# Residual input turned by DMA ahead of time instead of by TensorE; another order of VectorE's steps in the output projection; wider row sums

## The reference, cut to what matters

```
h = rmsnorm(x) ; all projections = h @ w_in
branch a: short convolution ; branch b: windowed attention ; branch c: attention over the top 256 keys
merged = sig(g_a)*br_a + sig(g_b)*br_b + sig(g_c)*br_c
x = x + merged @ w_out                 # output projection and residual
h2 = rmsnorm(x)
x = x + (silu(conv(h2 @ w_gate)) * (h2 @ w_up)) @ w_down
y = rmsnorm(x)                         # row by row, output in rows
```

## Time and profile before

| | |
|---|---|
| Time, median of 3 runs | 1747.86 us (1747.72 to 1748.6) |
| The profiled execution's own time | 1749.35 us |
| Its span in the trace | 1747.6 us |
| PE busy | 1716.7 us, 98% |
| DVE, ACT, POOL busy | 77%, 43%, 33% |
| Granted TensorE clock, mean | 0.998 |
| DMA engines busy, over the whole span | 27% |

### The profile page before, as it was taken

The page is one execution under the profiler, slowest core; times in us unless marked ns, Lnnn a source line. Parts: engine busy times, 40 slices in busy tenths (PEclk is TensorE's granted clock), DMA queues, the critical chain, the costliest instruction groups (busy, mean ns, idle before and its releaser), DMA issues.

```text
span 1747.6 us, 32318 instructions
## 1 busy us (share of the span) xinstructions
PE 1716.7 (98%) x12275; PEld 1676.9 (96%) x12275; DVE 1345.7 (77%) x2193; ACT 757.3 (43%) x1333; POOL 580.1 (33%) x466
## 2 busy tenths in 40 slices
PE   6999999999999999999999999999999999999998
PEld 6999999999999999888899999999999999999998
DVE  6689899978799996778659989676666665865765
ACT  5344333378621234767734563333333333422334
POOL 2211842266645431000021102655455554121030
PEclk9999999999999999999999999999999999999999
DMA  4111111110243415422324112222222223533212
GB/s 157 49 26 42 50 43 48 49 41 26 72 133 127 125 40 171 144 85 85 109 71 150 49 49 61 87 84 76 74 80 79 87 74 107 171 117 112 62 37 100
DMA packets 179190, 146.43 MB, mean 84 GB/s; under 512 B 10140, under 2 KB 149676, under 8 KB 179052
## 3 DMA queue, kind: packets, MB, share of 16 engines
q1 hardware_dynamic: 178076, 142.54, 26.2%
q0 software_dynamic: 976, 2.00, 0.5%
HBM read 118.22 MB, written 26.28 MB: 83 GB/s over the span
## 4 chain that ended last, share of the span: by engine, by line
PE 87%; DVE 5%; ACT 2%; POOL 2%; issue 2%; DMA 1%; SPq 0%; DVEq 0%; ACTq 0%; POOLq 0%
PE ps L1602 28%; PE ps L2079 23%; PE ps L2152 7%; PE ps L2138 7%; PE ps L1775 4%; PE ps L1795 4%; PE ps L1614 4%; PE ps L2009 3%; PE ps L1921 3%; PE ps L1869 1%; POOL w_lo L1332 1%; PE ps L1714 1%; POOL w_raw_in_lo L1345 1%; PE ps L1876 1%; DMA w_raw<-in_w_in 1%
## 5 line engine op out<-in xcount | busy, mean ns | idle before, releaser
L3178 DVE MAX8 top<-key_mask 128x8 f32<-128x1024 f32 (+5 forms) x166 | 151.9, 917 | 9.7 <-DVE key_mask L3178 3.4
L1602 PE MATMUL ps<-h_hi,w_hi 128*128 128x352 f32 (+1 forms) x720 | 158.0, 327 | 0.0
L1602 PE MATMUL ps<-h_hi,w_lo 128*128 128x352 f32 (+1 forms) x720 | 155.2, 323 | 0.0
L1602 PE MATMUL ps<-h_lo,w_hi 128*128 128x352 f32 (+1 forms) x720 | 154.8, 323 | 0.0
L1289 POOL TENSOR_TENSOR w_lo<-w_raw,w_hi 128x512 fp32r<-128x512 f32 (+1 forms) x43 | 79.3, 1845 | 216.9 <-ACT w_hi L2246 216.9
L3178 DVE MATCH_REPLACE8 key_mask<-top,key_mask 128x1024 f32<-128x1024 f32 (+5 forms) x166 | 149.5, 904 | 0.3 <-issue 0.3
L2079 PE MATMUL ps<-mix_hi,quarter_hi 128*128 128x264 f32 x672 | 136.9, 285 | 0.3 <-ACT x_one L2246 0.3
L2079 PE MATMUL ps<-mix_hi,quarter_lo 128*128 128x264 f32 x672 | 136.4, 284 | 0.0
L2079 PE MATMUL ps<-mix_lo,quarter_hi 128*128 128x264 f32 x672 | 136.0, 284 | 0.0
L1602 PEld LDWEIGHTS ps<-h_hi,w_hi 128*128 128x128 f32 (+1 forms) x720 | 120.6, 187 | 2.6 <-issue 0.9
L1602 PEld LDWEIGHTS ps<-h_hi,w_lo 128*128 128x128 f32 (+1 forms) x720 | 122.5, 186 | 0.5
(11 more groups left out here) (452 smaller groups left out, 5018.1 us busy)
## 6 DMA issues: line engine op xcount, KB each, us to landing
w_raw<-in_w_in SPq DMA_DIRECT2D x54, 256.0 KB, 3.1
w_hi<-gate_highs SPq DMA_DIRECT2D x48, 256.0 KB, 2.8
w_lo<-gate_lows SPq DMA_DIRECT2D x48, 256.0 KB, 3.0
ffn_tiles<-t SPq DMA_DIRECT2D x44, 264.0 KB, 2.4
w_raw<-in_w_gate SPq DMA_DIRECT2D x44, 256.0 KB, 3.1
w_raw<-in_w_up SPq DMA_DIRECT2D x44, 256.0 KB, 3.1
w_raw_in_lo<-in_w_in SPq DMA_DIRECT2D x30, 256.0 KB, 3.0
w_raw<-in_w_down SPq DMA_DIRECT2D x32, 192.0 KB, 2.8
```

Source lines behind the costliest of these rows:

```text
L1602: last = nc.tensor.matmul(PS[0:rows, NB * k + b, 0:e - a], w[:, k, t, 0:rows], x[:, t, a:e], start=m == 0 and w is WHI and x is hi, stop=m ...
L3178: step.mark(V_.max(top, s) if find else V_.match_replace(s, top, s, TAKEN))
```

## The change

**Residual.** The second load of x, the nine groups of transposes on PE and ACT's nine copies are gone. Instead, during the gates of the second branch, SP turns x by DMA. A float32 is taken as two 16-bit halves. In turn j, two transposing DMAs (`x_turn`) take the 128 features of tile j (256 halves) of the 1024 prompt rows and of the 32 sample rows into `x_halves_turned`. One DMA stores this to DRAM (`x_bounce`, 540 KB) and another loads it again in another layout (`x_plane_load`, 540 KB), so that a partition holds the low halves of its feature and then the high halves. ACT interleaves the halves again (`x_column`, one copy of 2112 16-bit elements on each partition), and SP stores the finished tile (`x_store`, 540 KB). `x_column(j)` stands one turn after `x_turn(j)`, and `x_store(j)` two turns after. The rest of the last tiles is done while the third branch's weights load, and ACT waits for all eight stores before it copies K to place 38, which the turned halves used. In the output projection SP loads the eight finished tiles into the residual, and VectorE waits for these (`xr_in`).

**Order on VectorE.** In the output projection `mix_t_raw(4)` stands behind the first low halves, `out_low(1, S2)` and `out_add(1, A11)` stand ahead of `residual(1)`.

**Row sums.** Each matmul of the last norm's row sums takes the column of ones 32 times: it writes 32 equal columns, of which one is read. ACT squares the last tile two rows of y sooner, and VectorE adds the last quarter product before it scales the late rows.

```
+            def x_turn(j):
+                at = bass.ds(j * (2 * P), 2 * P)
+                sp.dma_start_transpose(X_TURNED[:, :, 0:SEQ], x_halves(ins["x_prompt"])[:, at]).then_inc(xt_turned, 16)
+                sp.dma_start_transpose(X_TURNED[:, :, SEQ:TOK], x_halves(ins["x_sample"])[:, at]).then_inc(xt_turned, 16)
+            def x_bounce(j):
+                sp.wait_ge(xt_turned, 32 * j + 32)
+                sp.dma_start(X_HALVES[at, :].rearrange("(c p) t -> p c t", p=P), X_TURNED[:, :, :]).then_inc(xt_halves, 16)
+            def x_plane_load(j):
+                sp.wait_ge(xt_halves, 16 * j + 16)
+                sp.dma_start(X_PLANES[:, :, :], X_HALVES[at, :].rearrange("(p h) t -> p h t", h=2)).then_inc(xt_planes, 16)
+            def x_store(j):
+                sp.wait_ge(xt_columns, landed(j + 1))
+                sp.dma_start(X_TILES[bass.ds(j, 1), :, :].rearrange("a p t -> p (a t)"), X_COLUMNS[:, :]).then_inc(xt_stored, 16)
...
+                first_loads(1)
+                second_loads(1)
+                third_load(1)
+                sp.wait_ge(pv_done, WINDOW[-1]["q"] + len(WINDOW[-1]["chunks"]))
+                x_turn(0)
+                x_bounce(0)
+                x_plane_load(0)
+                x_turn(1)
+                with sp.Fori(2, KT) as j:
+                    first_loads(j)
+                    second_loads(j)
+                    third_load(j)
+                    x_bounce(j - 1)
+                    x_store(j - 2)
+                    x_plane_load(j - 1)
+                    x_turn(j)
+                x_bounce(KT - 1)
...
                 for k in range(2):
                     free(n0, 0, k)
                     load(k, plain(k, columns(w_in, kv[k])))
+                    if n0 == J_C and k == 0:
+                        x_store(KT - 2)
+                        x_plane_load(KT - 1)
                 if n0 == J_C:
                     gate_store(KT - 1)
+                    x_store(KT - 1)
...
-            sp.wait_ge(job_done, J_WO - 1)
-            for i in range(0, NT, 2):
-                src = ins["x_prompt"][0, i * P:(i + 2) * P, :].rearrange("(t p) d -> p t d", p=P)
-                sp.dma_start(XR[:, i:i + 2, :], src).then_inc(xr_in[i // 2], 16)
+            def residual_load(j):
+                sp.wait_ge(sum_ready, max(SPARSE_ORDER.index(j), SPARSE_ORDER.index(j // 2)) + 1)
+                sp.dma_start(X2[:, j, :], X_TILES[j]).then_inc(xr_in[j // 2], 16)
+            sp.wait_ge(xt_stored, landed(16 * KT))
+            for j in (0, 1, 3, 2):
+                residual_load(j)
...
-            project(J_WO, 0, 0, M_HI, M_LO, ready=(m_lo, 0), order=SPARSE_ORDER,
-                    between={t: x_tile(t - 3) for t in range(3, KT)})
-            project(J_WO, 0, 1, M_HI, M_LO, between={t: x_tile(t + 5) for t in range(4)})
+            project(J_WO, 0, 0, M_HI, M_LO, ready=(m_lo, 0), order=SPARSE_ORDER)
+            project(J_WO, 0, 1, M_HI, M_LO)
...
-                    sums = nc.tensor.matmul(PS[0:rows_of(i), bank, i:i + 1], squares[:, i * P:i * P + rows_of(i)],
-                                            ONES[:, :], start=first and i == rows[0], stop=last, skip_group_check=True)
+                    sums = nc.tensor.matmul(PS[0:rows_of(i), bank, WIDE * i:WIDE * (i + 1)],
+                                            squares[:, i * P:i * P + rows_of(i)],
+                                            ONES[:, 0:1].broadcast_to([P, WIDE]),
+                                            start=first and i == rows[0], stop=last, skip_group_check=True)
...
+            def x_column(j):
+                act.wait_ge(xt_planes, landed(16 * j + 16))
+                act.wait_ge(xt_stored, landed(16 * j))
+                copy(X_COLUMNS[:, :].bitcast(U16).rearrange("p (t h) -> p t h", h=2),
+                     X_PLANES[:, :, :].rearrange("p h t -> p t h")).then_inc(xt_columns, 1)
...
+                gate(0)
+                with act.Fori(1, KT) as j:
+                    gate(j)
+                    x_column(j - 1)
+                x_column(KT - 1)
...
-            for i in range(NT + 1):
-                r = rows_of(i)
-                act.wait_ge(xr_t, i + 1)
-                src = PS[:, 6:8, :].rearrange("p b (j t) -> p (b j) t", t=P)
-                copy(X2[:, :, i * P:i * P + r], src[:, :, 0:r]).then_inc(xr_out, 1)
...
-            dve.wait_ge(xr_out, 5)
-            mix_t_raw(4)
-            dve.wait_ge(xr_out, NT + 1)
```

More of the change, by code:

```diff
@@ L807, in y_banks, with sums_of @@
             return PS[0:rows_of(i), first:first + 2, :].rearrange("p b n -> p (b n)")
+        WIDE = 32
+        def sums_of(rows, bank, a, b):
+            return PS[0:rows, bank, 0:WIDE * (NT + 1)].rearrange("p (i n) -> p i n", n=WIDE)[:, a:b, 0]
         def y_count(i):
@@ L1061, in gate_loads, with first_loads @@
                 sp.dma_start(GATE_RAW[:, :, :], columns(w_in, C_G + 2 * D)).then_inc(sparse_raw, 16)
-                with sp.Fori(1, KT) as j:
+                def first_loads(j):
                     free(n0, j, 0)
@@ L1142, in _ @@
                         sp.dma_start(dst, src).then_inc(out_in[half], 16)
+                if m == 1:
+                    for j in range(4, KT):
+                        residual_load(j)
             sp.wait_ge(pair_lo, out_count(OUT_PAIRS[-1], Q_A22))
@@ L1983, in _ @@
                 project(0, n // 2, n % 2, O_HI, O_LO, tiles=CT, pieces=ROUNDS)
-            def x_tile(i):
-                def run():
-                    pe.wait_ge(xr_in[i // 2], 16)
-                    pe.wait_ge(xr_out, i)
-                    r = rows_of(i)
-                    for j in range(KT):
-                        transpose(PS[:, 6 + j // 4, (j % 4) * P:(j % 4) * P + r],
-                                  XR[0:r, i, j * P:(j + 1) * P], xr_t if j == KT - 1 else None)
-                return run
-            project(J_WO, 0, 0, M_HI, M_LO, ready=(m_lo, 0), order=SPARSE_ORDER,
-                    between={t: x_tile(t - 3) for t in range(3, KT)})
-            project(J_WO, 0, 1, M_HI, M_LO, between={t: x_tile(t + 5) for t in range(4)})
+            project(J_WO, 0, 0, M_HI, M_LO, ready=(m_lo, 0), order=SPARSE_ORDER)
+            project(J_WO, 0, 1, M_HI, M_LO)
             def out_product(m, q, hi, lo, first=False, mix=None):
@@ L4089, in _ @@
                         square_sum(KT, SQ[:, 0:HALF], 0, HALF)
+                    add(m, q)
+                    if m == last and q == Q_A22:
                         scales(LATE_ROWS, 1)
-                    add(m, q)
                     following_lows(m, i)
```

44 lines of the change are left out of this document (31 added, 13 removed).

## The result

The changed kernel takes 1751.53 us (median of 21 runs, 1750.51 to 1754.75), the kernel before in the same comparison 1748.45 (1747.65 to 1751.21). The ratio is 1.0019, with a 95% interval of 1.0013 to 1.0025: 3 us slower. I had forecast 1744.2, 4 us faster.

What follows compares the result with a forecast made beforehand. TensorE was taken to bound the kernel, with VectorE next in the output projection. 1749.35 - 1.75 - 1.7 - 0.2 = 1745.7 us profiled, less 1.49 gives a median of 1744.2; range 1742.5 to 1762.

Steps and rivals of the forecast that it cites:

- I take 2 us for both: SP's queue in the gates: issuing the two transposing DMAs takes 2 us together, from bounds of 0.41 to 1.0 each.
- In each turn, T + 3.9 + 0.8 must be under 17.48: Gates, each turn: transfer, store landing and issues must fit TensorE's turn, which allows T up to 12.8 us.
- T: Time of a transposing DMA in the gates: taken as 4.5 us, between 3.6 and 13.6, no cost under 6.5.
- From 557.3 there are 6.9 us for the issue of two transposing DMAs: SP's queue in the gates: room of 6.9 us before the next turn's `w_raw<-in_w_in` must go out at 564.2.
- 6.9 us are free, each beyond is paid in seven turns: SP's queue in the gates: issue time beyond 6.9 us costs that excess in each of seven turns.
- the signs that I had named: Signs included T under 6.5 us and issues under 3 each; ACT or TensorE waiting for `w_raw` each turn would refute it.
- The rival on the other side: SP's queue, gates: transposing DMA outlasts its lead, 1764 us at T = 13.6; chance 0.14 for 7 to 14, 0.11 longer.
- ACT's copy: Gates: one copy of 2112 elements per turn, 1.96 us within 3.75 us of ACT's idle time, costing nothing.
- Before K: Third branch: K's weights load behind the last turned tile, wanted at 603.74, which allows T up to 6.5 us.
- the walk given for K and V: Third branch's start: V split after 613.1 instead of 608.60, last store landed at 617, K copied at 620.19; nothing lost.
- The output projection: Removed transposes free 7.8 us of TensorE; VectorE leaves 1.75 gained (bounds 0.5 to 3.4), waits 2.3 at S2, 2.0 at S4.
- The end: Row sums of 32 columns keep TensorE's clock, gaining 1.7 us at even chances; two shifts of order give 0.2.

Runs made afterwards that it cites:

- the first experiment: Changed kernel with the store of the turned halves (`x_bounce`) moved ahead of the loads of `w_swa_o` in SP's loop of the gates: 1745.63 us, ratio to before 0.9983.
- four turns in place of one: Against the first experiment, the 1024 prompt rows are turned by four transposing DMAs of 256 rows instead of one: 1748.29 us.
- c3_narrow_only: Against the first experiment, the row sums at the end write one column instead of 32, new order at the end kept: 1745.87 us.
- s4_narrow_sums: Against the changed kernel, the row sums at the end write one column instead of 32: 1751.16 us.

## Why the prediction was wrong

**The stage of the gates is where it failed**: the term "I take 2 us for both", the two transposing issues, which take 4.5 to 5.0 us, and the test that should have caught it. That test was the step "In each turn, T + 3.9 + 0.8 must be under 17.48", with the one before it, "From 557.3 there are 6.9 us for the issue of two transposing DMAs". Each was true of one transfer. Neither added up SP's own turn. SP's program is a chain of its own, twelve issues (two each for `w_raw<-in_w_in` and `w_swa_o`) and two waits for the landing of its own stores. By the rows of after it is

- `gate_w_raw`, store of the halves and of the column, wait for the halves: 577.03 to 582.93, 5.9
- planes and the two transposing issues: to 589.21, 6.3
- `w_raw`, the two stores, `w_swa_o`: to 593.7, 4.5
- the wait for the stores: to 595.70, 2.0

18.7 us against TensorE's 17.48. I had the first, third and fourth in my rows, and the second as 0.4 + 2. With my numbers (issue 2, landings 3.9) the sum is 4.7 + 3.0 + 4.5 + 1.1 = 13.3, and it would have fitted, but it would have shown 4.2 us of room for both issues and landings together, not 6.9 for the issues alone. The terms that were off: the two issues, 5.0 us in this turn and 4.5 by their medians, where I took 2, which was also my upper bound; and the landings of stores beside the new traffic, 4.8 and 4.7 us instead of 3.9:

```profile
x_halves<-x_halves_turned SPq DMA_DIRECT2D x8, 528.0 KB, 4.8
...
gate_lows<-gate_w_lo SPq DMA_DIRECT2D x8, 512.0 KB, 4.7
...
x_halves_turned<-in_x_prompt SPq DMA_TRANSPOSE x8, 5.3
x_halves_turned<-in_x_sample SPq DMA_TRANSPOSE x8, 2.3
```

The landings are some 2 us of the difference of 5.4, the issues 3. So the bound on the issue was too low because I took the issue time of plain DMAs for that of a transposing one; "6.9 us are free, each beyond is paid in seven turns" gave the wrong point of decision. The four experiments settle it: 4 us of wait out, 3.5 of issue out, all out: each 5.7 to 6.0 us less; a store of 1.5 us in each turn in: 11.7 more. Two of the signs that I had named had come: an issue over 3 us, and ACT waiting for `w_raw` in the turns.

**T was right**: 5.3 us for the 1024 rows, 2.3 for the sample, by their medians (from below 3.6, taken 4.5, and no cost under 6.5); in the first experiment 6.2, near the bound. 21 us, the estimate from the Trainium skill, VectorE: DVE Perf Modes, section The three transpose paths, is four times what these rows measure for one long DMA. The Trainium skill, Advanced Engine Details and Errata, section X-Bar Transpose (TRN2), says that such a DMA is as fast as a regular one. The rows come near that: `gate_w_raw` with as many bytes lands in 4.1 us in this kernel, and the plain loads in the place of the transposing ones in 4.5. The rival on the other side had the right place, SP's queue between `gate_w_raw` and `w_raw`. It counted the issue too, but with 6.9 us free it could not see one of 5.0.

One sum of that rival is too high. At T = 13.6 a turn is 18.3 us, 0.8 over and not 1, so it comes to 18.7 us instead of 20; and at T = 13, the end of the range, to 13.9, which is 1758 and not 1762. Nothing hangs on it.

**ACT's copy**: 2.21 us instead of 1.96, hidden as said.

**Before K**: ACT split K's weights at 612.62 instead of the 603.74 it had been given, since SP was 8.7 us late by then (`gate_w_raw` at 595.70 against 587.02). Where SP keeps its turn, the walk given for K and V holds: K is copied at 620.32 in the first experiment, 620.19 before.

**The output projection** was right. 7.8 us go, the waits of 2.3 at S2 (2.21) and a late S4 came, and VectorE's work bounded the gain; I took 1.75, measured are 2.4, within the bounds. The wait at S4, 2.0 forecast and 0.24 measured, was hidden in the clock that fell after the wait at S2, which I had not expected and which cost nothing, since VectorE was late anyway: with four turns in place of one the clock stayed, and S4 waited 1.69. That more than 1.75 could be had lies in VectorE's steps: two low halves of the third mixture took 2.54 us before (968.27) and 1.28 in the first experiment. GpSimd was at work beside them in both, so its part in this is not shown.

**The end** was right in the profile and wrong in the time. 1.76 us come in the trace, but the medians show 0.2 to 0.3 for it, and the reason given, the narrow sums, is not shown: with the new order the clock stayed with one column too (c3_narrow_only, s4_narrow_sums). A clock dip read from one execution was taken as one of every execution, and the chance I gave it was one of "falls or not", where it is a share of the executions.

Both parts together, 2.8 us (1745.5 against 1748.3), would have been "the same" by the bound of 3.5 us. I had forecast 3.7 us of gain, so 0.9 of it was missing even where SP's turn fits.

## What to carry to other kernels

Where steps are added to a queue's loop, add up that queue's own turn, issues and waits for its own transfers, and compare it with the bottleneck's; slack of the single transfer doesn't tell. A wait right behind a transfer's issue costs the queue its whole landing, so put the store first and other issues between it and its wait: one line moved was worth 5.9 us here and left the kernel 2.7 us faster than before. A dip of the clock in one profile says nothing of its price in the median: ask how many runs have it.

## What the runs showed of the hardware

A transposing DMA of 16-bit values cost SP 3.2 to 3.8 us to issue for 1024 rows of 512 bytes in the changed kernel and 3.1 to 5.4 in the first experiment, and 1.2 us for 32 or 256 rows, against 0.4 for a plain one of 512 KB. It landed 5.3 us after the start of its issue (6.2 in the first experiment). The DMA engines were busy to 0.89 for 120 us beside TensorE at full rate, and TensorE waited for nothing. After 2.2 us of idle in the output projection TensorE ran at full clock for 1.3 us and then at half clock for 3.4; in the first experiment the same wait is followed by a fall too (0.93 granted from 950 to 975), and in the kernel with four turns it is not (1.00 from 970.0 to 974.9). So the same wait at the same place was followed by a fall in one execution and not in another.
